# Sample states in two buffers and scaled on ScalarE, with a new order of the first tiles, of the first sixteen FFN products and of the keys

## The reference, cut to what matters

```python
h = _rmsnorm(x, g_pre_mix)
aq, ak, av, rq, rf, ri, rg = jnp.split(h @ w_in, SPLIT_POINTS, axis=-1)
a = attention(q, k, v, window=128, sinks)
f = lb + (1.0 - lb) * jax.nn.sigmoid(rf)
kr, qr = 1.0 - f, jax.nn.silu(rq)
S_new = f * S + kr (outer) ri          # one step per sample row, in chunks for the prompt
o = qr @ S_new                          # normalized and gated by silu(rg)
mix = jnp.concatenate([a, o], axis=-1) @ w_out
x = x + _rmsnorm(mix, g_post_mix)
h2 = _rmsnorm(x, g_pre_ffn)
ffn = (jax.nn.silu(h2 @ w_gate) * (h2 @ w_up)) @ w_down
x = x + _rmsnorm(ffn, g_post_ffn)
```

## Time and profile before

| what | value |
|---|---|
| median of 3 runs | 1227.59 us (1227.31 to 1230.76) |
| the profiled execution | 1227.49 us, its span 1225.7 us |
| TensorE busy | 1201.1 us, 98% |
| VectorE busy | 876.6 us, 72% |
| ScalarE busy | 485.9 us, 40% |
| GpSimd busy | 229.2 us, 19% |
| mean granted clock of TensorE | 0.993 |
| DMA | 169.82 MB, mean 139 GB/s |

### The profile page before, as it was taken

How to read it: one execution, slowest core, us unless ns; L and a number is a source line. 1 busy time by engine, 2 the same in 40 slices (tenths; PEclk the granted TensorE clock), 3 DMA queues, 4 the chain that set the end, 5 groups by cost and what they waited for, 6 DMA issues and landing times.

```text
span 1225.7 us, 23606 instructions
## 1 busy us (share of the span) xinstructions
PE 1201.1 (98%) x9397; PEld 1186.5 (97%) x9397; DVE 876.6 (72%) x1525; ACT 485.9 (40%) x997; POOL 229.2 (19%) x162
## 2 busy tenths in 40 slices
PE   9999999999999999998999999999999999999997
PEld 9899999999998999998999999999999999999996
DVE  4877566573747685789877888888888575567676
ACT  6643543625140364455422322222222335455542
POOL 1000010101010000000023255657664220000011
PEclk9999999999998999999999999999999999999999
DMA  9431100105264442234355465867675376686466
GB/s 305 107 91 36 36 19 1 37 18 88 37 106 69 106 160 83 70 96 130 87 163 162 160 208 188 265 218 241 203 246 187 125 230 203 201 256 190 142 154 118
DMA packets 174014, 169.82 MB, mean 139 GB/s; under 512 B 23144, under 2 KB 126328, under 8 KB 173376
## 3 DMA queue, kind: packets, MB, share of 16 engines
q1 hardware_dynamic: 171728, 164.78, 45.4%
q0 software_dynamic: 2176, 3.52, 1.8%
HBM read 116.73 MB, written 52.58 MB: 138 GB/s over the span
## 4 chain that ended last, share of the span: by engine, by line
PE 61%; DVE 5%; issue 1%; ACT 0%; DVEq 0%; ACTq 0%
PE pair L1808 33%; PE pair L1848 18%; PE pair L1767 6%; PE pair L1548 3%; DVE mix L2289 1%; DVE mix L2314 1%; DVE w_lo L2247 1%; DVE qinv L2285 1%; PE pair L1739 0%; PE pair L1680 0%; PE pair L1750 0%; DVE act_lo L2297 0%; DVE mix L2452 0%; DVE acc L2351 0%; DVE mix L2272 0%
## 5 line engine op out<-in xcount | busy, mean ns | idle before, releaser
L1808 PE MATMUL pair<-act_hi,w_hi 128*128 128x258 f32 x704 | 199.6, 284 | 4.3 <-DVE w_lo L2247 2.7
L1808 PE MATMUL pair<-act_hi,w_lo 128*128 128x258 f32 x704 | 198.9, 283 | 0.0
L1808 PE MATMUL pair<-act_lo,w_hi 128*128 128x258 f32 x704 | 198.7, 282 | 0.0
L1848 PE MATMUL pair<-a_ring,w_hi 128*128 128x258 f32 x1056 | 189.6, 283 | 0.6 <-DVE mix L2452 0.5
L1548 PE MATMUL pair<-act_hi,w_hi 128*128 128x344 f32 x528 | 177.8, 337 | 0.2 <-DVE w_lo L1921 0.2
L1548 PE MATMUL pair<-act_hi,w_lo 128*128 128x344 f32 x528 | 170.0, 322 | 0.0
L1548 PE MATMUL pair<-act_lo,w_hi 128*128 128x344 f32 x528 | 169.7, 321 | 0.0
L1848 PEld LDWEIGHTS pair<-a_ring,w_hi 128*128 128x128 f32 x1056 | 162.5, 189 | 1.6 <-DVE mix L2452 0.9
L1808 PE MATMUL pair<-s_hi,w_lo 128*128 128x258 f32 x528 | 149.3, 283 | 0.0
L1808 PE MATMUL pair<-s_hi,w_hi 128*128 128x258 f32 x528 | 149.2, 283 | 0.0
L1808 PE MATMUL pair<-mix_r,w_hi 128*128 128x258 f32 x528 | 149.0, 282 | 0.0
(11 more groups left out here) (323 smaller groups left out, 2639.3 us busy)
## 6 DMA issues: line engine op xcount, KB each, us to landing
raw<-w_up_dram SPq DMA_DIRECT2D x26, 512.0 KB, 5.1
a_in<-h_sums SPq DMA_DIRECT2D x44, 258.0 KB, 3.4
rawx<-w_gate_dram SPq DMA_DIRECT2D x22, 512.0 KB, 4.8
w_quarter<-w_down_dram SPq DMA_DIRECT2D x44, 256.0 KB, 3.9
w_sums<-w_quarter SPq DMA_DIRECT2D x44, 256.0 KB, 4.6
rawx<-w_sums SPq DMA_DIRECT2D x44, 256.0 KB, 3.8
raw<-w_in_dram SPq DMA_DIRECT2D x18, 512.0 KB, 4.4
h_scratch<-mix SPq DMA_DIRECT2D x23, 258.0 KB, 2.1
```

The lines of the kernel that those rows point to most:

```text
L1808: mm = pe.matmul(pair[psum_pair(n)][:, s, 0:QW], a[:, r, half + k, :], b, start=(k == 0 and i == 0), stop=(k == 3 and i == 2))
L1848: mm = pe.matmul(dpair(mt)[:, s, 0:a.shape[1]], b[:, cut], a, start=(m == 0 and n == 0), stop=(m == HALVES - 1 and n == 2))
```

## The change

- The start: weights 0 and 1 are loaded and split in halves, between the pieces of x; `keep_warm(18)` in place of 30; `weight_hi(2)` ahead of `row_squares(0)`. The low part of the first queries is made at tick 10, ahead of two unit reads.
- Sample states: two buffers (the second, `st_odd`, where `kst` lay). States 0 and 1 are loaded one after the other at tick 96; state h + 2 is loaded after the store of state h, at the tick of `r_o(h)`. The scaling is eight ScalarE instructions in place of one on GpSimd. Ticks are written out: `r_scale` 97, 101, 105, 117, `r_sum` 98, 103, 106, 118, `r_o` 100, 105, 108, 120.
- Keys: `key_rows` comes ahead of the other recurrence steps of its tick; `f_s` is copied there, behind `hk`; `prep` waits for `f_gate`.
- The first sixteen FFN products: `L(2)` goes from product 10 to 11, behind `X(7)`; `X(5)` goes ahead of the reads of product 7; the low part of the last `h2` goes behind those of product 8; the weight of `X(5)` is loaded ahead of the first store of `h`.
- The last rows: the gain is multiplied on ScalarE (`y_gains`), VectorE only adds x, two tiles at a time.

```diff
-SR0, SRS = 99, 6
+R_SCALE, R_SUM, R_OUT, R_TURN = (97, 101, 105, 117), (98, 103, 106, 118), (100, 105, 108, 120), 123
...
-            8: [("S", 1, 1), ("S", 3, 1)], 9: [("X", 6), ("S", 2, 1), ("S", 4, 1)], 10: [("L", 2)], 11: [("X", 7), ("L", 1)],
+            8: [("S", 1, 1), ("S", 3, 1)], 9: [("X", 6), ("S", 2, 1), ("S", 4, 1)], 11: [("X", 7), ("L", 2), ("L", 1)],
...
+    st_odd, _ = at("st_odd", [P, DECB, P], F32, region)
+    sts = (st, st_odd)
...
-        load_weight(0)
+        load_weight_part(0, 0)
         load_x(0, 2, 4)
+        load_weight_part(0, 1)
         load_x(0, 4, 6)
         load_x(0, 6, 8)
-        load_weight(1)
+        load_weight_part(1, 0)
+        load_weight_part(1, 1)
...
-                    if h:
-                        sp.wait_ge(sem("s_o"), h)
-                        sp.wait_ge(sem("st_out"), 16 * h)
-                    else:
+                    if h == 0:
                         sp.wait_ge(sem("at_out"), NITEM)
-                    sp.dma_start(st[:], t_in["state_hgrn"][0, :, h].rearrange("b k v -> k b v")).then_inc(sem("st_in"), 16)
+                        load_state(0)
+                        sp.wait_ge(sem("s_mm"), 1)
+                        load_state(1)
             for step in sample_steps(tick):
                 if step[0] == "r_o":
                     h = step[1]
                     sp.wait_ge(sem("s_state"), h + 1)
-                    sp.dma_start(t_out["st_s"][0, :, h].rearrange("b k v -> k b v"), st[:]).then_inc(sem("st_out"), 16)
+                    sp.dma_start(t_out["st_s"][0, :, h].rearrange("b k v -> k b v"), sts[h % 2][:]).then_inc(sem("st_out"), 16)
+                    if h + 2 < NREC:
+                        sp.wait_ge(sem("s_o"), h + 1)
+                        sp.wait_ge(sem("st_out"), 16 * (h + 1))
+                        load_state(h + 2)
...
+        ffn_raw(5, 0, True)
         store_h(0, "11")
-        ffn_raw(5, 0, True)
...
-                    pool.tensor_tensor(st[:], st[:], bc(f_s[:, h, :].unsqueeze(2), [P, DECB, P]), ALU.mult).then_inc(sem("st_scaled"), 1)
...
+                    for b in range(DECB):
+                        ins = act.activation(sts[h % 2][:, b, :], sts[h % 2][:, b, :], ACT.Copy, scale=f_s[:, h, b:b + 1])
+                    ins.then_inc(sem("st_scaled"), 1)
...
+            act.wait_ge(sem("f_gate"), 2 * CH * (h + 1))
             act.activation(hk[:], r_f[:, 0:SEQ], ACT.Identity, scale=-1.0, bias=1.0).then_inc(sem("hk_prep"), 1)
+            copy(f_s[:, h, :], r_f[:, SEQ:ROWS]).then_inc(sem("f_done"), 1)
...
             for step in recurrence_steps(tick):
+                if step[0] == "prep":
+                    key_rows(step[1])
+            for step in recurrence_steps(tick):
                 h = step[1]
...
-        keep_warm(30)
+        keep_warm(18)
...
             if tick == 10:
                 first_low(2, range(KT))
+                query_low(0)
...
+            if n == 7:
+                job_low(("X", 5))
             ffn_reads(n)
+            if n == 8:
+                h2_low(QUADS - 1, 1)
...
-                for i in range(k, k + 4):
-                    y = yo[:, i, block_rows(3)]
-                    dve.scalar_tensor_tensor(out=y, in0=y, scalar=gain[:, POST_FFN, i:i + 1], in1=x_last[:, i, :],
-                                             op0=ALU.mult, op1=ADD).then_inc(sem("y_t"), 1)
+                for i in range(k, k + 4, 2):
+                    dve.tensor_tensor(yo[:, i:i + 2, block_rows(3)], yo[:, i:i + 2, block_rows(3)], x_last[:, i:i + 2, :], ADD)\
+                        .then_inc(sem("y_t"), 2)
```

More of the change, by code:

```diff
@@ L524, in build, with split_count @@
         raw_count.append(slot_total[n % 2])
+    def split_count(n, part=1):
+        return 2 * n + part + 1 if n < 2 else n + 3
     def unit_of(u):
@@ L618, in sample_steps @@
         for h in range(NREC):
-            d = tick - (SR0 + SRS * h)
-            out += [(s, h) for s, v in (("r_scale", 0), ("r_outer", 2), ("r_o", 4)) if d == v]
-        d = tick - (SR0 + SRS * NREC)
+            out += [(s, h) for s, v in (("r_scale", R_SCALE), ("r_sum", R_SUM), ("r_o", R_OUT)) if tick == v[h]]
+        d = tick - R_TURN
         out += [(s,) for s, v in (("r_rows", 0), ("r_cols", 2)) if d == v]
@@ L1017, in _ @@
                     h = step[1]
-                    pool.wait_ge(sem("f_done"), h + 1)
+                    pool.wait_ge(sem("f_gate"), 2 * CH * (h + 1))
                     if h:
@@ L1117, in weight_hi, with weight_hi_part @@
             copy(hi, raw[:, n % 2]).then_inc(sem("w_hi_done"), 1)
+        def weight_hi_part(n, part):
+            act.wait_ge(sem(f"w{n}_in" if part else f"raw_in{n}"), 16)
+            ks = slice(4 * part, 4 * part + 4)
+            copy(w_tiles(n)[0][:, ks], raw[:, n, ks]).then_inc(sem("w_hi_done"), 1)
         def root(out, in_, scale, done, value):
@@ L1150, in _ @@
         first_high(0, range(0, 2))
-        weight_hi(0)
-        first_high(0, range(2, 8))
-        weight_hi(1)
+        weight_hi_part(0, 0)
+        first_high(0, range(2, 4))
+        weight_hi_part(0, 1)
+        first_high(0, range(4, 8))
+        weight_hi_part(1, 0)
+        weight_hi_part(1, 1)
         act.wait_ge(sem("const_set"), 3)
+        weight_hi(2)
         row_squares(0)
-        weight_hi(2)
         row_squares(1)
@@ L1177, in forget_gate @@
             act.activation(z, z, ACT.Identity, scale=lbt[:, 5, m:m + 1], bias=lbt[:, 6, m:m + 1]).then_inc(sem("f_gate"), 1)
-            if c == CH - 1:
-                act.wait_ge(sem("f_gate"), 2 * n + 2)
-                copy(f_s[:, m, :], r_f[:, SEQ:ROWS]).then_inc(sem("f_done"), 1)
         def key_rows(h):
@@ L1289, in _ @@
                     copy(irow[:, 4 * a:4 * a + 4, :], BR.rearrange("p (b d) -> p b d", b=4)).then_inc(sem("i_rows"), 1)
-                if step[0] == "prep":
-                    key_rows(h)
                 if step[0] == "ot":
@@ L1373, in y_root, with y_gains @@
             bank_root(act, block_part(ystd, b), bank[:, 0:BLOCKS[b][1]], "y_stat", b + 1).then_inc(sem("y_std"), 1)
+        def y_gains(ks):
+            for k in ks:
+                x = yo[:, k, block_rows(3)]
+                ins = act.activation(x, x, ACT.Copy, scale=gain[:, POST_FFN, k:k + 1])
+            return ins
         def job_high(job):
@@ L1531, in _ @@
                 y_squares("21", 1)
+                y_gains(range(0, 4)).then_inc(sem("y_sq"), 1)
             if v == FULL + HALVES + 5:
@@ L1537, in _ @@
         y_root(3)
+        y_gains(range(4, KT)).then_inc(sem("y_sq"), 1)
     @blk.tensor
@@ L1600, in _ @@
                     b0, nb = V_GROUPS[step[1]]
-                    pe.wait_ge(sem("unit_act"), unit_index("v", 0, 1 if step[1] == 0 else 2) + 1)
+                    pe.wait_ge(sem("unit_act"), (unit_index("ri", 0, 1) if step[1] == 0 else unit_index("v", 0, 2)) + 1)
                     take_br("v_rows", step[1] + 1)
@@ L1950, in _ @@
         first_low(0, range(0, 2))
-        weight_lo(0)
-        first_low(0, range(2, 8))
-        weight_lo(1)
+        weight_lo_part(0, 0)
+        first_low(0, range(2, 4))
+        weight_lo_part(0, 1)
+        first_low(0, range(4, 8))
+        weight_lo_part(1, 0)
+        weight_lo_part(1, 1)
         weight_lo(2)
@@ L2071, in mix_low, with query_low @@
                                   act_hi[:, 4 * kk:4 * kk + 4, cols(c)].bitcast(F32), ALU.subtract).then_inc(sem("mix_lo"), 1)
+        def query_low(i):
+            t, j, e = i // NBLK, i % NBLK, i % 2
+            dve.wait_ge(sem("q_high"), i + 1)
+            dve.tensor_tensor(q_lo[:, e, :], mix[:, t, P * j:P * j + P], q_hi[:, e, :].bitcast(F32), ALU.subtract)\
+                .then_inc(sem("q_low"), 1)
         for tick in range(TICKS):
@@ L2093, in _ @@
                 k0 = WIN if j == 0 else 0
-                if step == "Q":
-                    dve.wait_ge(sem("q_high"), i + 1)
-                    dve.tensor_tensor(q_lo[:, e, :], mix[:, t, P * j:P * j + P], q_hi[:, e, :].bitcast(F32), ALU.subtract)\
-                        .then_inc(sem("q_low"), 1)
+                if step == "Q" and i:
+                    query_low(i)
                 elif step == "S":
@@ L2124, in _ @@
                 if step[0] == "prep":
-                    dve.wait_ge(sem("f_done"), h + 1)
+                    dve.wait_ge(sem("f_gate"), 2 * CH * (h + 1))
                     if h:
@@ L2203, in _ @@
                     ins.then_inc(sem("s_vec"), 1)
[L2204 removed]
+                if step[0] == "r_sum":
                     h = step[1]
@@ L2424, in _ @@
                     sum_low(*step[1:])
-                if step[0] == "h2" and step[2]:
-                    h2_low(step[1], 1)
         def down_steps(n):
```

45 lines of the change are left out of this document (30 added, 15 removed).

## The result

The changed kernel takes 1232.68 us (median of 18 runs, 1230.53 to 1236.96); the kernel before, in 18 runs beside it, 1229.59 us (1225.29 to 1235.5). The ratio is 1.0026, with a 95% interval of 1.0014 to 1.0038: some 3.2 us slower, a small loss, but not chance. The forecast was 1226.5 us with a range from 1218 to 1231.

What follows compares the result with a forecast made beforehand. TensorE, busy for 98% of the span, was taken as the bound. Terms -1.0 - 1.0 + 0.4 - 6.6 + 5.8 + 0.6 + 1.5 - 0.7 = -1.0 us on 1227.49 gave 1226.5 us, range 1218 to 1231.

Steps and rivals of the forecast that it cites:

- 4, weight 19: SyncE queue behind the state stores: weight 19 lands near 358.2 us and holds ScalarE, VectorE and TensorE; +5.8 us.
- The second stop: Behind late weight 19: after stopping 3.3 us for unit 51, TensorE stops again until 367.7 us for `orn`.
- Rival B: Weight 19 is not late because the store or save ends sooner; -6.8 us, 1220.7 us; chance 0.30.
- Rival C: Stops at ticks 106 to 109 bring a lasting slow clock; 4.3 us more, 1230.8 us; chance 0.10.
- 3, the levels: Level products of head 3: without the `st` sum ahead, the `hk` wait and slow clock go; -6.6 us.
- 1, the first tiles: Kernel start: second x chunk about 0.8 us earlier, `q_lo` wait mostly replaced by one for `diag`; -1.0 us.
- 3 again, GpSimd at nothing: Sample states: GpSimd's scaling goes, no gain priced; ScalarE's eight products, 1.7 us per head, hidden except for head 2.
- 2 and 6: Keys: `hk` no longer delayed by the `irow` copy, -1.0 us; tail: two additions replace four gain products, -0.7 us.
- 5, the FFN: First FFN products: product 14 later by 0.6 us waiting for `u_tmp`, plus one slow-clock stretch of 1.5 us.

Runs made afterwards that it cites:

- halves_alone: Kernel before with only the half weights, 18 warm-up products and weight 2 ahead of the first squares, `query_low(0)` not moved; ratio 1.0033, +4.1 us.
- halves_whole_loads: halves_alone with weights 0 and 1 each loaded by one transfer, still split in halves by ScalarE and VectorE; ratio 1.0018 to the kernel before, +2.2 us.
- start_alone: Kernel before with only the first-tile edits: half weights, 18 warm-up products, `query_low(0)` moved, weight 2 ahead of the first squares; ratio 1.0026, +3.2 us.
- query_alone: Kernel before with only `query_low(0)` moved ahead of two unit reads and `k_lo`; ratio 1.0002, +0.2 us.
- w19_early: Changed kernel with the load of weight 19 issued at tick 99, before the waits of the state stores; ratio 0.9978 to the kernel before, -2.7 us.
- w19_before_save: Changed kernel with the load of weight 19 directly ahead of the save of `i_s` for head 2; ratio 1.0001 to the kernel before, +0.1 us.
- w19_w20_early: Changed kernel with weights 19 and 20 both loaded at tick 99, before the waits of the state stores; ratio 0.9958 to the kernel before, -5.2 us.
- states_keys_tail_early: Kernel before with the sample-state, keys and tail edits, weights 19 and 20 loaded at tick 99, no start or FFN edit; ratio 0.9946, -6.6 us.
- scale0_scalar: Kernel before with head 0's sample state scaled by ScalarE at tick 100, heads 1 to 3 still on GpSimd; ratio 0.9990, -1.2 us.

## Why the forecast was wrong

The forecast of -1.0 us became +3.1 in the traces, 4.1 us off by the terms below; the other 2.1 us are the starting value.

**4, weight 19: right.** Issue, landing, who is held and for how long came out within a few tenths, and undoing it gives back 5.9 us. The second stop, for `orn` until 367.7, didn't come: TensorE had its products at 1.2 GHz to do (20 of them took 0.29 us each), and the low clock filled the time. The sum was the same, and that was not luck, because the chain on ScalarE and VectorE that the forecast went through ends it either way. `orn` and `hk` in after:

```profile
366.28 1.29 DVE L2228 TENSOR_TENSOR hk<-pair,orstd 128x512 f32<-128x512 f32 x2
373.46 1.07 ACT L1206 ACTIVATE hk<-r_f 128x1024 f32<-128x1024 f32 x1
```

`orn` is done at 367.6 us (forecast 367.7) and `hk` at 374.5 (374.1), and the diagonal products start at 374.75. Rival B, weight 19 not late, fell. Rival C, the low clock at the stops, did happen, for 5.9 us and inside this term, not on top of it; that the measured median lies nearest to C's 1230.8 us is a coincidence.

**3, the levels: the step that failed.** The `st` sum is out of the way and the 10 us at 0.50 are gone, both as said. What the forecast left out, and put at nothing without a word, is what is late next in the same queue: weight 20, issued behind the wait for the sum of state 2 and its store. It brought a wait of 1.48 us back where the forecast had "Without it `hk` is ready as TensorE arrives", the term came out at -5.0 and not -6.6 us, and early weights 19 and 20 together gain 2.5 us more than 19 alone. The forecast asked only of weight 19 what the queue does to it. The `krow` wait of 0.5 us at 409 us comes too, in every kernel with the states' edit; what makes it late wasn't tried.

**1, the first tiles: the second step that failed**, and in sign. "It can't keep that: the second chunk of x lands at 24.69 us, behind the same bytes as before" took the landing for fixed or earlier. It was 1.0 us later in after (0.8 us by the middle profiles), and by the median the halves cost 4.1 us where 0.8 us of gain were forecast. At the ledger's first point (59.98 us before, 60.30 after) the eight profiles without any start edit lie at 58.50 to 60.81 us, halves_alone at 62.92 and halves_whole_loads at 61.92, and the five with the whole start edit at 60.30 to 60.84. So no gain came, but most of the 3.2 us that start_alone loses by the median doesn't show by 60 us, and where it lies stays open. The new wait for `diag` (2.13 us, forecast 2.1) and the 0.38 us left for `q_lo` (forecast half a microsecond) were right, and so was the remark that this is no gain: query_alone is at +0.2.

**3 again, GpSimd at nothing.** Its removal was costed at no time. The traces show it holding VectorE; the net value isn't told apart from zero. ScalarE's eight scalings take 2.44 us per head and not 1.7: they start 0.3 us apart and not 0.2, as the 0.3 us copies of 128 x 128 in the trace of before already suggested. That changed no term noticeably, since `hk` was still done at 374.5.

**2 and 6.** Keys: -1.0 forecast, -1.0 in the ledger; TensorE's waits for the key rows go from 2.1 to 1.0 us. Tail: VectorE is done 0.6 us sooner after the last product (6.9 us against 7.5), as forecast, but the stores ended later, and over the seven profiles with this edit the end comes 10.3 us after the start of the last product, against 10.5 in the eleven without it: 0.2, not 0.7. From profile to profile that distance varies by 0.5 to 0.7 us, and the +0.4 of the ledger is within it. The landing of the stores is what ends the kernel: in after VectorE's last operation ends 3.7 us before the span does.

**5, the FFN: a term mis-sized.** Forecast +2.1, ledger +1.1. The wait for `u_tmp` was 0.61 and not 2.4 us, since the low clock came ahead of it; in w19_early, with the clock up, it was 2.14.

The number 1226.5 was low by 2.1 us of starting value and by three small terms that all went one way: first tiles (+1.3), weight 20 with `krow` (+2.4), and the stores (+1.1), with +0.3 at `r_sum(0)` and -1.0 in the FFN beside them.

## What to carry to other kernels

When a wait is put into an in-order DMA queue, walk down all that is queued behind it until the first load that would have been waited for anyway, not only to the next one: here two late weights, worth 7.1 us in the states' edit alone, ate the 4.8 us that it gains without them. The cure was to issue them ahead of the wait, one line. And judge a change of 0.3% by parts: parts that gain and parts that lose looked together like one edit that does little.

## What was not expected of the hardware

**A load behind the save of 4-byte elements.** Weight 19 took 13.0 us from issue to copy behind it and 6.3 us ahead of it, issued at nearly the same time. The forecast had this from the earlier trace rows; the pair shows that most of it is the order. The save itself, 4 KB, landed 11.3 us after its issue in after and 12.0 us in w19_before_save.

**The same wait, with and without a low clock.** The same wait of 2.13 us for `diag` was followed by a low clock in w19_early (52.2 to 55.8 us), start_alone and query_alone, and not in after, w19_before_save and w19_w20_early. The wait of 2.93 us for `q_lo` in states_keys_tail_early was not followed by one, the same wait in halves_alone was. In scale0_scalar it fell at 318 us with no wait over 1 us ahead. So a slow stretch seen in a single profile is no price: the next execution may not have it. The spread between runs of one kernel goes with the mean granted clock: the runs of before at 0.995 took 1225 to 1227 us, the one at 0.986 took 1234.5.
